# First FFN of a two-layer token backbone on one core: w1 and w3 as seven products of half blocks, w2 on token halves in six row groups

## What is computed

```python
f_l = rmsnorm(x, norm_ffn_g[i]) * (1.0 + sc2) + sh2
x = x + g2 * swiglu(f_l, ffn_w1[i], ffn_w3[i], ffn_w2[i])
h_ctx = h_ctx + cg2 * swiglu(f_c, ffn_w1[i], ffn_w3[i], ffn_w2[i])   # layer 0 only
def swiglu(h, w1, w3, w2):
    return (jax.nn.silu(h @ w1) * (h @ w3)) @ w2
```

## Time and profile before

| | |
|---|---|
| median of 3 runs | 1680.38 us (1680.29 to 1681.06) |
| profiled execution, span of its instructions | 1679.1 us (no other time is given for it; 1.3 us under the median) |
| PE busy | 1613.2 us, 96% |
| DVE, ACT, POOL busy | 598.2, 520.8, 599.4 us (31 to 36%) |
| granted TensorE clock, mean | 0.987 |
| first FFN, end of the first w1 chunk's slot to last w2 matmul | 474.35 to 1042.96 us of the span |

### The profile page before, as it was taken

How to read it: one execution, slowest core, us unless ns; L and a number is a source line. 1 busy time by engine, 2 the same in 40 slices (tenths; PEclk the granted TensorE clock), 3 DMA queues, 4 the chain that set the end, 5 groups by cost and what they waited for, 6 DMA issues and landing times. The chain is left out here.

```text
span 1679.1 us, 22699 instructions
## 1 busy us (share of the span) xinstructions
PE 1613.2 (96%) x10014; PEld 1351.4 (80%) x10014; DVE 598.2 (36%) x713; ACT 520.8 (31%) x577; POOL 599.4 (36%) x433
## 2 busy tenths in 40 slices
PE   6999999998899999999999999999978999999997
PEld 4888787877788888888888887788866788888886
DVE  4553333453431121111211124769987322121122
ACT  4343242322321211111101123477873321122222
POOL 2121211212142332332323334345474444555443
PEclk7999999999999999999999999999999999999999
DMA  9333334222233432333332422121213233223322
GB/s 336 97 98 105 88 90 126 76 76 76 75 101 101 120 95 87 97 105 101 101 100 76 120 82 76 51 76 56 71 50 100 76 100 101 88 90 99 100 82 82
DMA packets 200341, 160.64 MB, mean 96 GB/s; under 512 B 7234, under 2 KB 193972, under 8 KB 200244
## 3 DMA queue, kind: packets, MB, share of 16 engines
q1 hardware_dynamic: 199856, 159.08, 30.7%
q10 hardware_dynamic: 388, 0.12, 0.0%
HBM read 157.08 MB, written 2.10 MB: 95 GB/s over the span
## 5 line engine op out<-in xcount | busy, mean ns | idle before, releaser
L512 POOL TENSOR_TENSOR w_lo<-raw,w_hi 128x512 fp32r<-128x512 f32 x392 | 561.3, 1462 | 1027.9 <-ACT w_hi L1063 1027.8
L574 PE MATMUL duo<-a_hi,w_hi 128*128 128x512 f32 (+1 forms) x1584 | 466.3, 356 | 23.2 <-DVE a_lo L1544 16.2
L577 PE MATMUL duo<-a_lo,w_hi 128*128 128x512 f32 (+1 forms) x1584 | 461.0, 353 | 0.0
L580 PE MATMUL duo<-a_hi,w_lo 128*128 128x512 f32 (+1 forms) x1584 | 460.5, 352 | 0.0
L1063 ACT ACTIVATE w_hi<-raw 128x2048 fp32r<-128x2048 f32 x98 | 187.6, 1914 | 539.8 <-PE duo L580 533.8
L574 PEld LDWEIGHTS duo<-a_hi,w_hi 128*128 128x128 f32 x1584 | 257.9, 190 | 77.0 <-issue 32.2
L577 PEld LDWEIGHTS duo<-a_lo,w_hi 128*128 128x128 f32 x1584 | 257.7, 190 | 42.8
L580 PEld LDWEIGHTS duo<-a_hi,w_lo 128*128 128x128 f32 x1584 | 257.3, 190 | 42.7
L1777 DVE TENSOR_TENSOR hid<-duo,gate 128x1024 f32<-128x1024 f32 (+1 forms) x33 | 33.5, 1043 | 523.3 <-PE duo L580 523.3
L574 PE MATMUL duo<-h_hi,w_hi 128*128 128x512 f32 (+1 forms) x528 | 160.5, 356 | 0.0
L580 PE MATMUL duo<-h_hi,w_lo 128*128 128x512 f32 (+1 forms) x528 | 159.4, 354 | 0.0
(11 more groups left out here) (275 smaller groups left out, 1591.9 us busy)
## 6 DMA issues: line engine op xcount, KB each, us to landing
raw<-in_ffn_w_dram SPq DMA_DIRECT2D x120, 512.0 KB, 4.8
mod_ring<-in_w_mod_dram SPq DMA_DIRECT2D x80, 512.0 KB, 5.4
raw<-in_gla_w_in_dram SPq DMA_DIRECT2D x24, 512.0 KB, 4.8
mod_start<-in_w_mod_dram SPq DMA_DIRECT2D x8, 1024.0 KB, 12.6
raw<-in_lru_w_in_dram SPq DMA_DIRECT2D x16, 512.0 KB, 4.1
raw<-in_ffn_w_dram SPq DMA_DIRECT2D x16, 384.0 KB, 3.8
raw<-in_gla_w_out_dram SPq DMA_DIRECT2D x8, 512.0 KB, 4.9
raw<-in_lru_w_out_dram SPq DMA_DIRECT2D x8, 512.0 KB, 4.0
```

Source lines behind the costliest of these rows:

```text
L512: pool.tensor_tensor(w_lo[b][:, k:k + 2], raw[b][:, k:k + 2], w_hi[b][:, k:k + 2].bitcast(F32), ALU.subtract).then_inc(lo_ready, 1)
L574: pe.matmul(tile_out(ps, t, part, n), wh, act_hi[:, k, s:s + n], start=opens, stop=False, skip_group_check=True)
L577: pe.matmul(tile_out(ps, t, part, n), wh, act_lo[:, k, s:s + n], start=False, stop=False, skip_group_check=True)
L580: mm = pe.matmul(tile_out(ps, t, part, n), wl, act_hi[:, k, s:s + n], start=False, stop=last, skip_group_check=True)
```

## The change

**Products.** Chunk pair 0 (w1 and w3, the first 256 hidden columns) stays as it was. For the 20 other chunks, the chunk's weight is taken as a 2x2 of half blocks (4 row tiles x 128 columns), the activations as a 2x2 of (4 row tiles x 384 tokens: half of the latent and half of the context tokens), and the result as 2 tiles x 2 token halves. Seven block products (`PRODUCTS`: A11, S2, S1, S3, A12, A22, S4) take the place of eight; each is 4 rows x 3 matmuls of 384 columns, 84 per chunk. S1 to S4 are sums of weight blocks, made by DVE per chunk (`weight_sum`, four TENSOR_TENSOR of 512 elements); the four sums of activation blocks are made once by DVE (`block_sums`), rounded by ACT and split by DVE (`block_low`).

**Accumulation.** The three banks of `duo` are written by products 0 and 4 (bank 0), 1, 3, 5 (bank 1), 2 and 6 (bank 2), adding up without a clear. Between them ACT copies bank 0 once and DVE adds banks into `gate` or `hid` (`after_product`); PE's products 3 to 6 wait for these reads.

**Weights.** They come as half chunks of 4 row tiles (512 KB) into four quarter buffers. A piece (4 rows x 128 columns) is rounded by ACT (`high_piece`) into a ring of five, five products ahead of PE; its remainder is made by POOL, or by DVE for S2 and S4 (`low_piece`). SP loads a half chunk when the one four places before has been summed and split (`quarter_free`).

**w2** runs in six row groups: hidden pair 0 alone, then two pairs each. A w2 piece is one output tile of the group's rows; its matmuls are 384 columns wide, two token halves. The tile sums are added to `xres` per group. In the last group, tile 7's second half is split into 128 context and then 256 latent columns, and only the latter is done last.

**Order on the engines.** DVE and ACT each run one loop over all 188 pieces with a wait on `piece_used` per piece. The modulation slots, transposes and `half_section` calls stay with their chunks. In `prep(0, 1)` the normalised rows go to a buffer for all rows, and `a_hi`, `a_lo` are written in the order of the token halves; one small DVE instruction (`shift_gap`) is added before it.

The diff, cut to its core and moved left by 12 columns where it was nested (PE, SP, POOL first, then ACT, then DVE):

```diff
+RING = 5
+ROW_GROUPS = [[0], [1, 2], [3, 4], [5, 6], [7, 8], [9, 10]]
+def unit_list():
+    units = []
+    for group, pairs in enumerate(ROW_GROUPS):
+        for i in pairs:
+            for w in ("w1", "w3"):
+                if i:
+                    units.append((w, i))
+                if (w, i) == ("w1", 1):
+                    units.append(("w2", 0))
+        if group:
+            units.append(("w2", group))
+    return units
+UNITS = unit_list()
+PRODUCTS = [("A11", 0), ("S2", 1), ("S1", 2), ("S3", 1), ("A12", 0), ("A22", 1), ("S4", 2)]
+SUMS = ["S1", "S2", "S3", "S4"]
+BY_DVE = ("S2", "S4")
...
+def quarter_free(half):
+    n = HALF[half]
+    if n < 4:
+        sp.wait_ge(lo_ready, 4 * (CH[("w1", 0, 0) if n < 2 else ("w3", 0, 0)] + 1))
+        return
+    before = HALVES[n - 4]
+    if before[0] != "w2":
+        sp.wait_ge(sum_made, SUM_COUNT[before[:2] + (("S3", "S4")[before[2]],)])
+    for piece in pieces_of(before):
+        lo_wait(sp, piece)
...
+for g, piece in enumerate(PIECES):
+    if piece[2] not in BY_DVE:
+        pool.wait_ge(piece_hi, g + 1)
+        pool.tensor_tensor(piece_rows(ring_lo, piece), piece_source(piece),
+                           piece_rows(ring_hi, piece).bitcast(F32), ALU.subtract).then_inc(lo_by_pool, 1)
...
+    for j, (p, b) in enumerate(PRODUCTS):
+        lo_wait(pe, u + (p,))
+        if j == 0:
+            duo_wait(name)
+            if W1_BEFORE[u]:
+                pe.wait_ge(c11_taken, W1_BEFORE[u])
+        elif j == 1 and chunk == 0:
+            pe.wait_ge(t_ready, 4)
+        elif j == 3:
+            pe.wait_ge(bank_read, 3 * chunk + 1)
+        elif j == 4:
+            pe.wait_ge(first_copied, chunk + 1)
+        elif j == 5:
+            pe.wait_ge(bank_read, 3 * chunk + 2)
+        elif j == 6:
+            pe.wait_ge(bank_read, 3 * chunk + 3)
+        hi, lo = piece_rows(ring_hi, u + (p,)), piece_rows(ring_lo, u + (p,))
+        act_hi, act_lo = moving[p]
+        out_ = banks[:, b, 0:HT]
+        for k in range(4):
+            pe.matmul(out_, hi[:, k], act_hi[:, k], start=j < 3 and k == 0, stop=False, skip_group_check=True)
+            pe.matmul(out_, hi[:, k], act_lo[:, k], start=False, stop=False, skip_group_check=True)
+            mm = pe.matmul(out_, lo[:, k], act_hi[:, k], start=False, stop=k == 3, skip_group_check=True)
+        mm.then_inc(piece_used, 1)
...
+    second = range(2, 4)
+    for t in range(2):
+        down_begin(group, t)
+        pe.wait_ge(row_ready, 2 * pairs[0] + 2)
+        for h in range(2):
+            down_tile(group, t, first, h)
+    for t in range(2):
+        for h in range(2):
+            pe.wait_ge(row_ready, 2 * pairs[1] + h + 1)
+            mm = down_tile(group, t, second, h)
+        mm.then_inc(piece_used, 1)
...
+        if last and t == KT - 1:
+            down_tile(group, t, range(4), 1, slice(HL, HT)).then_inc(tile_done, 1)
+            mm = down_tile(group, t, range(4), 1, slice(0, HL))
+        else:
+            mm = down_tile(group, t, range(4), 1)
+        mm.then_inc(piece_used, 1)
...
+def first_ffn():
+    norm_sums(1, BOTH)
+    for m, name in enumerate((("w1", 0, 0), ("w3", 0, 0))):
+        tile_pair(name, name, BOTH, a_hi, a_lo, ready=a_wait(("prep", 0, 1)) if m == 0 else None)
+        section_slot(m)
+    for u in UNITS:
+        if u[0] == "w2":
+            down(u[1])
+        else:
+            seven_products(u)
+            section_slot(2 * u[1] + (u[0] == "w3"))
...
+def high_piece(piece):
+    g = PIECE[piece]
+    before = slot_before(g)
+    if before is not None:
+        act.wait_ge(piece_used, before + 1)
+    if piece[0] == "w2":
+        half_wait(act, piece[:2] + (piece[2] // 2,))
+    elif piece[2] in SUMS:
+        act.wait_ge(sum_made, SUM_COUNT[piece])
+    else:
+        half_wait(act, piece[:2] + (int(piece[2] != "A11"),))
+    act.activation(piece_rows(ring_hi, piece), piece_source(piece), ACT.Copy).then_inc(piece_hi, 1)
...
+    if j == 0:
+        if u[0] == "w1":
+            act.wait_ge(hid_made, 2 * pair - 1)
+        else:
+            act.wait_ge(row_ready, 2 * pair - 1)
+        act.activation(out_[:, 1, 0:HT], duo(name)[:, 0, 0:HT], ACT.Copy).then_inc(first_copied, 1)
+    elif u[0] == "w1" and j == 4:
+        act.activation(gate[:, 0, 0:HT], duo(name)[:, 0, 0:HT], ACT.Silu).then_inc(c11_taken, 1)
+    elif u[0] == "w1" and j == 5:
+        act.wait_ge(c21_made, chunk + 1)
+        steps.mark(act.activation(gate[:, 1], gate[:, 1], ACT.Silu))
+    elif u[0] == "w1" and j == 6:
+        wait_moved(act, name)
+        act.activation(gate[:, 0, HT:TOK], gate[:, 0, HT:TOK], ACT.Silu).then_inc(gate_made, 1)
+    elif j == 5:
+        row_rounded(pair, 0)
+    elif j == 6:
+        row_rounded(pair, 1)
...
+def block_sums(m):
+    sh = mod[:, 3]
+    n11, n12, n21, n22 = [normed_all[:, m, i] for i in range(4)]
+    both = ((0, slice(0, HL)), (1, slice(HL, HT)))
+    steps.link(dve.tensor_tensor(n11, n12, n11, ALU.subtract))
+    for part, cols in both:
+        steps.mark(dve.scalar_tensor_tensor(out=n12[:, cols], in0=n22[:, cols], scalar=shift_gap[:, m, part:part + 1],
+                                            in1=n12[:, cols], op0=ALU.add, op1=ALU.subtract))
+    for part, cols in both:
+        steps.mark(dve.scalar_tensor_tensor(out=n22[:, cols], in0=n22[:, cols], scalar=sh[:, m + 4, part:part + 1],
+                                            in1=n11[:, cols], op0=ALU.add, op1=ALU.subtract))
+    steps.wait()
+    for part, cols in both:
+        ins = dve.scalar_tensor_tensor(out=n21[:, cols], in0=n21[:, cols], scalar=sh[:, m + 4, part:part + 1],
+                                       in1=n22[:, cols], op0=ALU.add, op1=ALU.subtract)
+        if part == 0:
+            steps.mark(ins)
+    ins.then_inc(t_made, 1)
+def block_low(m):
+    dve.wait_ge(t_rounded, m + 1)
+    dve.tensor_tensor(t_lo[:, m], normed_all[:, m], t_hi[:, m].bitcast(F32), ALU.subtract).then_inc(t_ready, 1)
...
+def sums_for(piece):
+    if piece[2] == "S2":
+        weight_sum(piece[:2], "S1")
+        weight_sum(piece[:2], "S2")
+    elif piece[2] in ("S3", "S4"):
+        weight_sum(piece[:2], piece[2])
+def low_piece(piece):
+    if piece[2] in BY_DVE:
+        dve.wait_ge(piece_hi, PIECE[piece] + 1)
+        dve.tensor_tensor(piece_rows(ring_lo, piece), piece_source(piece),
+                          piece_rows(ring_hi, piece).bitcast(F32), ALU.subtract).then_inc(lo_by_dve, 1)
...
+    if j == 1:
+        dve.wait_ge(first_copied, chunk + 1)
+        dve.tensor_tensor(c12, b, c21, ALU.add).then_inc(bank_read, 1)
+    elif j == 3:
+        dve.tensor_tensor(c22, b, c21, ALU.add).then_inc(bank_read, 1)
+        dve.wait_ge(bank_read, 3 * chunk + 2)
+        dve.tensor_tensor(c22, c_, c22, ALU.add).then_inc(bank_read, 1)
+    elif j == 4 and u[0] == "w3":
+        dve.wait_ge(gate_made, pair)
+        steps.mark(dve.tensor_tensor(hid[:, 0, 0:HT], a, gate[:, 0, 0:HT], ALU.mult))
+    elif j == 5:
+        dve.tensor_tensor(c21, b, c21, ALU.add).then_inc(c21_made, 1)
+        if u[0] == "w3":
+            dve.wait_ge(c21_made, chunk + 1)
+            dve.wait_ge(bank_read, 3 * chunk + 3)
+            dve.tensor_tensor(hid[:, 1], hid[:, 1], gate[:, 1], ALU.mult).then_inc(hid_made, 1)
+    elif j == 6:
+        moved(dve.tensor_tensor(c12, c_, c12, ALU.add), name)
+        if u[0] == "w3":
+            wait_moved(dve, name)
+            dve.tensor_tensor(c12, c12, gate[:, 0, HT:TOK], ALU.mult).then_inc(hid_made, 1)
+            row_low(pair, 0)
+            if UNITS[UNITS.index(u) + 1][0] == "w2":
+                row_low(pair, 1)
...
+    dve.wait_ge(tile_done, 2)
+    steps.mark(add_down(5, t, 0, slice(0, 1), slice(0, 1)))
+    add_down(5, t, 1, slice(0, 2)).then_inc(tile_added, 1)
+    add_squares(2, 3, BOTH)
+    piece_wait(dve, ("w2", 5, t))
+    moved(add_down(5, t, 0, slice(1, 2), slice(2, 3)), name)
+    wait_moved(dve, name)
...
+def first_ffn():
+    block_sums(0)
+    block_sums(1)
+    block_low(0)
+    block_sums(2)
+    block_low(1)
+    block_sums(3)
+    block_low(2)
+    dve.wait_ge(mod_turned, 13)
+    block_low(3)
+    wait_done(dve, ("w1", 0, 0))
+    for piece in PIECES[0:RING + 1]:
+        sums_for(piece)
+    for piece in PIECES[0:RING - 1]:
+        low_piece(piece)
+    name = ("w3", 0, 0)
+    wait_moved(dve, ("w1", 0, 0))
+    wait_done(dve, name)
+    dve.tensor_tensor(hid[:, :, 0:LAT], part_psum(name, 0), gate[:, :, 0:LAT], ALU.mult).then_inc(hid_made, 1)
+    moved(dve.tensor_tensor(hid[:, :, LAT:TOK], part_psum(name, 1), gate[:, :, LAT:TOK], ALU.mult), name)
+    wait_moved(dve, name)
+    dve.memset(zero[:], 0.0).then_inc(hid_made, 1)
+    row_low(0, 0)
+    row_low(0, 1)
+    half_section(6, 0)
+    g = 0
+    for n, u in enumerate(UNITS):
+        for j in range(KT if u[0] == "w2" else len(PRODUCTS)):
+            if u != ("w2", len(ROW_GROUPS) - 1) or j < KT - 1:
+                dve.wait_ge(piece_used, g + 1)
+            if u[0] != "w2":
```

(30 more changed lines are left out.)

379 lines of the change are left out of this document (315 added, 64 removed).

## The result

The change makes the kernel slower: 1703.91 us as a median of 4 runs (1699.44 to 1704.65), beside 1680.72 (1680.29 to 1681.38) for the kernel before, measured with it. The ratio is 1.0128 [1.0112, 1.0145]. The forecast was 1652, the range 1638 to 1668, so sign and range were both missed. The profiled execution of the kernel after is the quickest of the four (1699.44 us) and has a span of 1697.5 us, 18.4 more than before.

What follows compares the result with a forecast made beforehand. PE's own work was taken to bound the first FFN. The terms -42.3 + 3.5 + 0.5 + 0.5 + 6 + 3 + 0.2 (split half's matmul starts) gave -28.6, taking the 1680.4 us median to 1652, range 1638 to 1668.

Steps and rivals of the forecast that it cites:

- the one on the queues: SP's load queue: same bytes, half chunks asked for about 15 us before needed, modulation ring wait harmless; cost nothing.
- Matmuls, -42.3: First FFN's 20 chunks: 240 matmuls removed, counted as 120 pairs at 0.3526 us each, saving 42.3 us.
- Rival 4: Products and w2: 384-column matmuls start every 0.19 us, not 0.176, costing 38 us; 1690 us, chance 0.03.
- DVE per chunk, +3.5: Full w3 chunks: PE's product 5 waits for DVE's bank addition, 0.7 us five times; +3.5 us (0 to 8).
- w2 entries, +0.5: Between a w3 chunk's last product and w2: DVE and ACT's hidden-row chain mostly hidden behind PE's work; +0.5 us.
- group 0, +0.5: w2 group 0: tiles last only 2.1 us while DVE adds additions to two sums at tile 3; +0.5 us (0 to 2).
- The start, +6: First w1 chunk after pair 0: DVE's activation sums and splits make PE wait at products 0/1 and 3; +6 us (0 to 9).
- The end, +3: Behind the last w2 matmul: tile additions and squares delay the norm's matmuls by 1.6 to 3.6 us more; taken as +3.
- the 536 to 541 named as a sign: Stage from the first w3 chunk to the end of w2: falls from 568.6 us to 536 to 541.
- The second (the shared port): Chunks, start and end: DVE becomes the bound through POOL contention; gain only 12 to 18 us, 1663 to 1668, chance 0.20.
- The third (three banks): Products 3 to 6: PE waits in all 20 chunks for late reads of three shared banks; slower, 1690 us, chance 0.05.
- The first (waits hidden): Whole stage: POOL and DVE miss each other, leaving -42.3 with 2 to 5 us of waits; 1640 to 1645, chance 0.20.

Runs made afterwards that it cites:

- the first experiment: The changed kernel with the two modulation loads for each slot before a w2 group issued ahead of that group's last w2 half chunk: 1645.25 us, ratio 0.9781.

## Why the prediction was wrong

**The step that failed is the one on the queues.** It said that SP's wait for the modulation ring "stands in front of" the half chunks "and lets go at the end of the chunk two earlier, which leaves the same 15. Nothing." It asked whether that wait delays the weights, between chunks that follow each other. It never asked the other way round: what do the modulation loads stand behind, where a w2 group lies between. That is also the place where the order was rewritten, from behind the first w2 chunk to behind the next chunk's halves. Priced at nothing, it costs 43.1 us of wait in five slots and 12 of slower clock in and behind them, 57.3 in the stage and 58.7 by the medians (1703.91 - 1645.25). No rival held it: all four looked for trouble in the products or their engines.

**Matmuls, -42.3.** Right in kind, and priced a little too dear: 384 columns start every 0.1733 us nearly throughout, the quick end of the range, as in the last w2 tiles below (11 starts in 1.91 us, 0.174 each). Over 2736 matmuls that is 8.2 us less than the 0.1763 that I took. Rival 4 is out.

```profile
1055.40 0.33 PE L1173 MATMUL duo<-ha_hi,ring_hi 128*128 128x384 f32 x1
...
1057.31 0.33 PE L1175 MATMUL duo<-ha_hi,ring_lo 128*128 128x384 f32 x1
```

**DVE per chunk, +3.5.** Smaller, and elsewhere. I put the wait at product 5 of a w3 chunk; there is none. PE waits at product 3 of the five w1 chunks that stand right behind a w3 chunk, 0.22 each, 1.1 in all (the row of the gate above, less the 2.3 of the start). DVE's load was sized too high, and its place was off: such a w3 chunk and the w1 chunk behind it, with their slots, were forecast at 25.4 to 31 us of DVE in 31.6, and DVE is busy for 21.9 of 31.4 (first row below); of these the w1 chunk alone has 11.4 in 15.3 (second row, another pair). Single terms were off both ways: `half_section` takes 0.9 us and not the 0.4, for which no row was given, and the second split of the hidden rows takes 2.0 beside POOL and not 0.96.

```profile
649.39:680.81 31.42, 31.20 (x206) 30.12 (x203) 21.85 (x28) 12.33 (x21) 12.86 (x9) 1.00 0.53 151
556.50:571.81 15.31, 15.09 (x90) 14.76 (x87) 11.36 (x13) 7.79 (x14) 7.14 (x5) 1.00 0.57 171
```

**w2 entries, +0.5, and group 0, +0.5.** One wait for `xres` of 0.5, in group 0: that term was right, and the entries cost nothing.

**The start, +6.** Too dear, with the chain as described: DVE's `block_sums` and `block_low` ran from 468.01 to about 489.5 (forecast 488.5 to 493), S2's remainder to 493.41, and product 1 did not wait; only product 3 did, for 2.30 us (forecast 2 to 6).

```profile
500.99 0.41 PE L1152 MATMUL duo<-t_hi,ring_hi 128*128 128x384 f32 x1 [2.30 <-DVE gate L2274]
```

**The end, +3.** The norm's matmuls are done 4.6 us after PE's last w2 matmul ends, against 2.9: +1.7, inside the forecast 1.6 to 3.6, at its low end. In the first experiment, where the norm's matmuls ran at half clock, it is 6.0, +3.1. That this meets the +3 forecast is luck: 1.4 of it is clock, which the forecast did not have.

```profile
1060.13 0.28 PE L1175 MATMUL duo<-a_hi,ring_lo 128*128 128x256 f32 x1
1063.05 1.53 PE L865 MATMUL duo<-sqsum_ffn,ones 128*128 128x256 f32 x4 [2.64 <-DVE sqsum_ffn L1869]
1064.42 0.59 PE L871 MATMUL duo<-sq,ones 128*128 128x256 f32 x2
```

**The rest of the sum.** With the queue mended the change is worth -36.7 where -28.6 was forecast, 1645.25 in a range of 1638 to 1668; the stage takes 528.9 us, below the 536 to 541 named as a sign. By terms: -42.3 - 8.2 for the matmuls; + 9.4 for all that PE's starts leave over the even spacing in the chunks and w2; + 3.1 at the end; 1.3 are left, spread over slots and changes of unit. The 9.4 stand beside 10.5 forecast for the four terms ahead of the end, and that is in part luck: only 3.3 of them are the waits named above, the other 6 are small delays of single starts, for which the forecast had no term.

**The rivals.** The second (the shared port) is real and small: some 5 us, by the version with all remainders on DVE, where I had priced the lost time at 10 and more. Its sum does not come out of its own terms either: taken as they stand, 5 to 10, 15, 9 and 4 make 33 to 38 us against the 42.3, which leaves -4 to -9 and not -12 to -18, so the upper end of the range rested on a slip. The third (three banks) fell with it: DVE took 69 us of work more and PE waited less. The first (waits hidden) is nearest to what the products do, but its 1640 to 1645 is met only with the queue mended (1645.25). What should have been a rival: the slots in front of w2 groups, five times (about 3 us until the queue lets go, 5.5 of landing, and the clock behind).

## What to carry to other kernels

For each load in an in-order queue, go through the order of issues at the places where the pattern changes, not only in its steady part, and ask what the last wait in front of it waits for; if that hangs on the work behind which the load is needed at once, the load is late by its whole landing time (5.5 us here), with the DMA engines a third busy. A load for a slot that comes soon belongs in front of those that wait for a ring; here it cost nothing to move it there. When a rewrite changes several things at once, price the moved issues with the same care as the removed matmuls: here two loads in the wrong place of the order, five times, cost 58.7 us and turned a gain of 36.7 into a loss.
